# A trunk in which GpSimd makes some low parts that VectorE made

## The reference

```
h = rms_norm(x);  z = h @ w_in + b_in                       # 1024 x 8448
oa = banded attention, 16 heads of 64 (sinks, partial rotary)
ob = spatial gating, 12 groups of 64 channels
oc = dilated attention, 4 heads x 3 groups, mixed by their log-sum-exp
merged = sig(g0)*(oa @ w_proj_a) + sig(g1)*(ob @ w_proj_b) + sig(g2)*(oc @ w_proj_c)
x = x + merged @ w_out
x = x + hier_moe(rms_norm(x))                               # 32 experts, top 1 group, top 2 in it
```

## Time and profile before

| | before |
|---|---|
| median of 3 runs | 1030.28 us (1030.17 to 1032.45) |
| the profiled execution | 1029.97 us |
| its span | 1028.3 us |
| TensorE busy | 961.8 us |
| VectorE busy | 575.5 us |
| ScalarE busy | 428.9 us |
| GpSimd busy | 58.1 us |

### The profile page before, as it was taken

How to read it: one execution, slowest core, us unless ns; L and a number is a source line. 1 busy time by engine, 2 the same in 40 slices (tenths; PEclk the granted TensorE clock), 3 DMA queues, 4 the chain that set the end, 5 groups by cost and what they waited for, 6 DMA issues and landing times.

```text
span 1028.3 us, 15490 instructions
## 1 busy us (share of the span) xinstructions
PE 961.8 (94%) x5906; PEld 670.8 (65%) x5906; DVE 575.5 (56%) x1184; ACT 428.9 (42%) x918; POOL 58.1 (6%) x74
## 2 busy tenths in 40 slices
PE   9999999999999995987999999999999999977877
PEld 7888877778886441533588887777788954344323
DVE  8656788896873231211276668898969533222212
ACT  5444566666443210210354355666664431111122
POOL 1120400000010000000004004000000100000000
PEclk9999999999999998998999999999999999989999
DMA  9975544247999999999998665342589999999996
GB/s 343 345 264 177 194 125 124 80 129 274 397 368 386 425 425 418 426 424 426 414 391 275 203 196 172 123 123 83 170 298 384 364 410 425 424 422 423 425 424 276
DMA packets 97114, 313.02 MB, mean 304 GB/s; under 512 B 13425, under 2 KB 18577, under 8 KB 74513
## 3 DMA queue, kind: packets, MB, share of 16 engines
q1 hardware_dynamic: 96704, 312.04, 80.0%
q10 hardware_dynamic: 336, 0.02, 0.0%
HBM read 310.20 MB, written 1.84 MB: 303 GB/s over the span
## 4 chain that ended last, share of the span: by engine, by line
PE 70%; DMA 10%; SPq 9%; DVE 6%; ACT 3%; issue 2%; POOL 0%; DVEq 0%; ACTq 0%; POOLq 0%
PE ps L1437 14%; PE ps L1439 14%; PE ps L1438 14%; SPq L484 9%; PE ps L2061 6%; DMA arena<-in_w_expert_up_dram 5%; DMA arena<-in_w_expert_gate_dram 3%; DMA ring_rest<-in_w_expert_down_dram 3%; PE ps L2147 2%; PE ps L2035 2%; PE ps L1462 2%; PE ps L2135 2%; ACT probs L966 2%; PE ps L1572 2%; PE ps L2006 1%
## 5 line engine op out<-in xcount | busy, mean ns | idle before, releaser
L1437 PE MATMUL ps<-whi,ahi 128*128 128x512 f32 (+1 forms) x736 | 284.4, 386 | 2.1 <-DVE arena L1109 1.1
L1090 DVE TENSOR_TENSOR wlo<-arena,whi 128x512 fp32r<-128x512 f32 (+1 forms) x352 | 233.0, 700 | 95.2 <-ACT whi L883 92.0
L1439 PE MATMUL ps<-whi,alo 128*128 128x512 f32 (+1 forms) x736 | 277.1, 377 | 0.0
L1438 PE MATMUL ps<-wlo,ahi 128*128 128x512 f32 (+1 forms) x736 | 276.8, 376 | 0.0
L883 ACT CAST whi<-arena 128x1024 fp32r<-128x1024 f32 (+1 forms) x171 | 175.5, 1028 | 176.6 <-PE ps L1439 168.0
L1437 PEld LDWEIGHTS ps<-whi,ahi 128*128 128x128 f32 x736 | 138.5, 188 | 31.1 <-issue 4.5
L1439 PEld LDWEIGHTS ps<-whi,alo 128*128 128x128 f32 x736 | 138.4, 188 | 25.6
L1438 PEld LDWEIGHTS ps<-wlo,ahi 128*128 128x128 f32 x736 | 138.7, 188 | 23.2
L2279 DVE SCALAR_TENSOR_TENSOR acts<-ps,wslot,acts 128x256 f32<-128x256 f32 x16 | 7.7, 484 | 169.9 <-ACT acts L1962 145.5
L2061 PE MATMUL ps<-arena,rows 128*32 128x512 f32 x416 | 90.7, 622 | 8.9 <-DMA arena<-in_w_expert_up_dram 7.3
L2061 PE MATMUL ps<-ring_rest,rows 128*32 128x512 f32 x352 | 76.6, 634 | 10.2 <-DMA arena<-in_w_expert_up_dram 10.2
(11 more groups left out here) (293 smaller groups left out, 1077.8 us busy)
## 6 DMA issues: line engine op xcount, KB each, us to landing
arena<-in_w_in_dram SPq DMA_DIRECT2D x62, 1024.0 KB, 5.4
arena<-in_w_expert_down_dram SPq DMA_DIRECT2D x38, 1024.0 KB, 20.5
arena<-in_w_expert_gate_dram SPq DMA_DIRECT2D x34, 1024.0 KB, 25.8
arena<-in_w_expert_up_dram SPq DMA_DIRECT2D x32, 1024.0 KB, 25.3
ring_rest<-in_w_expert_down_dram SPq DMA_DIRECT2D x24, 1024.0 KB, 18.9
ring_rest<-in_w_expert_gate_dram SPq DMA_DIRECT2D x22, 1024.0 KB, 25.8
ring_rest<-in_w_expert_up_dram SPq DMA_DIRECT2D x22, 1024.0 KB, 26.0
arena<-in_w_proj_a_dram SPq DMA_DIRECT2D x8, 1024.0 KB, 5.1
```

The source lines that it names most:

```text
L1090: dve.tensor_tensor(wlo[:, jj % 2, cols], half_slot(jj, w)[:, cols], whi[:, jj % 2, cols].bitcast(F32), ALU.subtract).then_inc(low_split i ...
L1437: pe.matmul(o, hi, rhs_hi, start=first, stop=False)
L1438: pe.matmul(o, hi, rhs_lo, start=False, stop=False)
L1439: return pe.matmul(o, lo, rhs_hi, start=False, stop=last)
```

## The change

GpSimd's list gets, behind the rotary work, six instructions in this order: `o_low(0)`, `o_low(1)`, `o_low(2)`, the second half of item 65's low part, that of item 66's, and `o_low(3)`. VectorE's list loses the same six (four of 128 x 512, two of 128 x 256, in each of the two layers); it keeps the first halves, keeps the fifth `o_low`, and gets a wait for `low_split` at 67 ahead of item 67 and a wait for `o_lo` at 4 ahead of the last `o_low`. SyncE's queue gets a second wait for the load of item 36. Helpers that only change their place in the file are left out below.

```diff
                             sp.wait_ge(low_split, 2 * (item - 4 + 1))
+                            if item == 36:
+                                sp.wait_ge(low_first, 2 * 33)
...
+                        def o_low(i):
+                            pool.wait_ge(o_hi, i + 1)
+                            pool.tensor_tensor(split_at(alo, i), o_blocks(i), split_at(ahi, i).bitcast(F32),
+                                               ALU.subtract).then_inc(o_lo, 1)
+
+                        def second_low(j):
+                            pool.wait_ge(hi_ready, j + 1)
+                            pool.wait_ge(low_split, j)
+                            cols = slice(TAIL, 2 * TAIL)
+                            pool.tensor_tensor(wlo[:, j % 2, cols], half_slot(j, TAIL)[:, cols],
+                                               whi[:, j % 2, cols].bitcast(F32), ALU.subtract).then_inc(low_split, 1)
+
+                        for i in range(3):
+                            o_low(i)
+                        second_low(65)
+                        second_low(66)
+                        o_low(3)
...
-                        def o_low(i):
-                            dve.wait_ge(o_hi, i + 1)
-                            dve.tensor_tensor(split_at(alo, i), o_blocks(i), split_at(ahi, i).bitcast(F32),
+                        def last_o_low():
+                            dve.wait_ge(o_hi, 5)
+                            dve.wait_ge(o_lo, 4)
+                            dve.tensor_tensor(split_at(alo, 4), o_blocks(4), split_at(ahi, 4).bitcast(F32),
                                               ALU.subtract).then_inc(o_lo, 1)
...
                             softmax_out(b + 1)
-                            low_at(47 + 2 * b)
+                            if b < BATCHES - 3:
+                                low_at(47 + 2 * b)
+                            else:
+                                low_half(65, TAIL, 66, 0)
                             if 1 <= b < 2 * TB:
                                 ln_apply(b)
-                            if b in SPLITS[:3]:
-                                o_low(SPLITS.index(b))
-
-                        softmax_in(BATCHES - 1, lambda: low_at(66))
+
+                        softmax_in(BATCHES - 1, lambda: low_half(66, TAIL, 67, 0))
+                        dve.wait_ge(low_split, 67)
                         low_at(67)
                         group_max(BATCHES - 1)
-                        o_low(3)
                         z_out(6, CHUNKS, TAIL, CHUNKS + 1, True)
...
                             if j == 70:
-                                o_low(4)
+                                last_o_low()
```

More of the change, by code:

```diff
@@ L796, in _, with o_at, o_blocks, split_at @@
                         load_ahead(9, 10)
+                    def o_at(p, n):
+                        at = ZQ + p * P if p < 8 else CQ + (p - 8) * P
+                        return z[:, :, at:at + n * P]
+                    def o_blocks(i):
+                        return o_at(2 * i, 2).rearrange("p t (k c) -> p k t c", k=2)
+                    def split_at(t, i):
+                        kb = 8 + 2 * i if i < 4 else 0
+                        return t[:, kb:kb + 2, :].rearrange("p k (t c) -> p k t c", t=TB)
+                    def half_slot(j, w):
+                        n = 2 * w
+                        return ring[:, (j // 2) % RING, (j % 2) * n:(j % 2) * n + n]
                     @block.gpsimd
@@ L854, in narrow_slot @@
                         return blocks[:, ks, c * (BANK // 2):(c + 1) * (BANK // 2)]
-                    def half_slot(j, w):
-                        n = 2 * w
-                        return ring[:, (j // 2) % RING, (j % 2) * n:(j % 2) * n + n]
                     @block.scalar
```

## The result

The changed kernel takes 1032.45 us (median of 22 runs, 1031.62 to 1034.29) against 1030.74 us of the kernel before in the same rounds (22 runs, 1029.51 to 1032.45). The ratio is 1.0014, 95% interval 1.0008 to 1.0020: slower by 0.8 to 2.1 us. That is less than the 0.3% which the prediction took as the least that can be told from no change, and the interval still keeps clear of 1. The profiled execution took 1032.62 us, its span 1030.9.

What follows compares the result with a forecast made beforehand. TensorE, busy 94% of the span, was taken as the bound. Losses of 0.50 + 0.42 = 0.92 us a layer, 1.84 in all, on 1029.97 us, plus 0.31 to the median, gave 1032.1 us; 8-in-10 range 1028.6 to 1034.3.

Steps and rivals of the forecast that it cites:

- The bound and the places that count: TensorE bounds; only o_low(2) (0.60 us) and the halves of items 65 and 66 (0.67 us) lie on its path.
- The price of a turn: GpSimd and VectorE instructions with two SBUF tensors exclude each other; VectorE loses up to 1.10 us per 128 x 512.
- a cheaper turn: Rival: contiguous operands let GpSimd go at its copy's 1.2 ns an element, giving 1030.3 us; 0.17, shared with no effect.
- Where each meets VectorE: Per layer, o_low(2) costs + 0.50 us in batch 6, each half + 0.21 in the last softmax, other o_low nothing.
- The margin: In the last softmax, o_low(3) fits beside VectorE's mask of 1.35 us and costs nothing, by some 0.1 us.
- the other side: Rival: o_low(3) falls ahead of a half of item 65 or 66, + 1.10 us a layer, 1034.3 us; chance 0.18.
- The new waits: VectorE's waits for item 66's half and the last o_low, and SyncE's before item 36's load, cost nothing.
- The sum: 0.50 + 0.42 = + 0.92 us a layer, 1.84 us for both, going through to the end: 1032.1 us.
- TensorE's idle time from 190 to 250 us: Sign: 1.38 us before; the prediction would be wrong if it fell.
- The case for a gain: Rival: GpSimd's work hides beside masks and reductions, gaining 1.27 us a layer, 1027.8 us; chance 0.15.
- Two rivals: GpSimd hides, or L1240 does not contend (1027.8 us, 0.15); contiguous operands make turns cheaper (1030.3, 0.17 with no effect).

Runs made afterwards that it cites:

- e7: Changed kernel with only o_low(0) and o_low(1) left on GpSimd, the other moved instructions back on VectorE: 1030.66 us, ratio 0.9999 to the kernel before.
- e3: Changed kernel with all four o_low on GpSimd and the two second halves back on VectorE: 1033.52 us, ratio 1.0029 to the kernel before.
- e2: Changed kernel with only the second halves of items 65 and 66 on GpSimd, all o_low back on VectorE: 1031.04 us, ratio 1.0001 to the kernel before.
- e4: Changed kernel plus waits in GpSimd's list, so its instructions start beside VectorE's masks, reductions or behind item 67's low part: 1027.94 us, ratio 0.9969 to before.
- e6: Changed kernel with o_low on GpSimd writing zeros instead of subtracting, so it reads nothing: 1031.49 us in its one run.

## Why the prediction was right

**The bound and the places that count.** Right: the moved instructions behind batches 4 and 5 cost VectorE 2.40 - 1.29 - 0.60 = 0.5 us each and the kernel nothing (e7); the other two places count in full.

**The price of a turn.** Taken as 2.15 ns an element from the rotary work (its rows gave 2.19 and 2.25), measured 2.1 (1.09 us for 512). The rows that it read had one turn in each pair; two other pairs of the rotary work, at 47.02 and 120.80 us in the trace of before, take 1.99 us, 0.71 more than alone, which is about the size of two turns. It holds for contiguous runs as for the rotary's runs of eight, which was the ground of the rival of a cheaper turn, and for L1240, which the trace of before had not shown beside GpSimd (1.96 for 1.43, and 0.95 for 0.42 for item 65).

**Where each meets VectorE.** Right in every case: one turn for `o_low(2)`, one for each half, none for `o_low(3)`, whose 1.47 us from 228.45 end at 229.92, before the mask does (230.04) and 0.04 us before item 66's first half starts (229.96). The margin was as thin as said: GpSimd's start was 0.25 us ahead of the mask's, while item 65's half still ran. That this one fell on the free side is in part luck; the prediction gave the other side 0.18, and e3 shows what one turn more costs. One thing was put too late: TensorE pays for the halves at the `turn_probs` of batch 10 and at item 65, not first at the last factor, and gets half of that back at item 67. The sum is the same, + 0.4 us.

**The new waits.** VectorE's is free, as said (e2). SyncE's was not tested by itself; in the 26.4 us behind L TensorE idles 0.25 us before and 0.23 in the changed kernel, so it costs nothing that can be seen there.

**The sum.** + 0.92 us a layer was forecast, + 0.90 and + 0.88 (38.85 against 741.33 - 703.36 = 37.97) are in the traces. That is 1.8 us for both; the runs say 1.4, between 0.8 and 2.1, and 1.7 by the two medians. The forecast's 1032.1 stood on a median of 1030.28 for the kernel before, which had 1030.74 in the rounds beside the changed kernel, so the miss of 0.35 is made up of 0.46 from there and a change forecast 0.1 too large. The shift does go through to the end: twice L's difference is + 3.1 us for e3 and - 2.6 for e4, and the runs say + 3.0 and - 3.2 (- 2.7 by the medians). Between the two L's, with the expert stage of layer 0 in it, the trace of before has 469.40 us and that of the changed kernel 469.31; behind the second they have 286.97 and 287.14. Tenths of a microsecond can't be settled there. TensorE's idle time from 190 to 250 us, whose fall would have spoken against the account, rose from 1.38 to 1.85 us.

**The case for a gain** was worked out at - 1.27 us a layer, and given 0.15. It did not come by itself, but e4 shows that its size was right, and that it needed only other starts. Two rivals fell by their ground: L1240 does contend (1.96 us for 1.43), and contiguous operands make a turn no cheaper.

## What to carry to other kernels

Before work goes from VectorE to GpSimd, list what VectorE does at the moment when the moved instruction will be released, and not how busy it is on the whole: a tensor by tensor operation in SBUF on GpSimd costs VectorE more (1.1 us here) than doing it itself (0.6 us) where VectorE stands in a run of two-tensor operations, and nothing where it reads PSUM, reduces or waits. A wait on a semaphore that VectorE signals anyway, put ahead of GpSimd's instruction, turns the one case into the other; here it turned a loss of 1.7 us into a gain of 2.7. And when a small effect drowns in the spread of whole runs, a length between two instructions of one trace shows it to some hundredths (here to 0.06 us from layer to layer), if both ends lie around every place that the change can touch.

## What the runs showed of the hardware

GpSimd holds VectorE up by what it reads: 2.1 ns an element for two tensors, 0.8 ns for one, nothing for writing alone (e6). It does so for 0.2 us less than its own row lasts: its free 512 elements last 1.29 us in the profile and hold for 1.09, those of a copy 0.62 and 0.41. The length of VectorE's instruction does not matter, six elements waited 1.1 us (e4). A run of VectorE instructions back to back does not keep GpSimd out, which gets its turn behind the one that is running: ahead of the second low part in the changed kernel (GpSimd's start at 197.32, VectorE's next at 197.36), and behind the second factor in e3 (226.67 and 226.60). The Trainium skill has the rule of two SBUF inputs against a GpSimd instruction that reads, and not against one that only writes (SBUF — State Buffer, "Who interferes with whom"); the traces agree with both halves of it.
